# Merging the two 64-key tails of a neighbourhood-attention value product into one block-diagonal matmul

## The reference

```
q, k, v = split(h @ w_qkv)                      # 16 heads of 64 features
# a query in grid column c sees all 8 rows and a clamped window of 16 columns
scores = q . k + bias[head, row offset, column offset]
p = softmax(scores)                             # over 8 x 16 keys
out = (p @ v) @ w_o
```

## Time and profile before

| | |
|---|---|
| three runs, us | 1041.26, 1042.48, 1043.23 (median 1042.48) |
| span of the profiled execution, us | 1041.8 |
| busy: PE, PE weight loads, DVE, ACT, POOL | 99%, 87%, 81%, 57%, 10% |
| attention loop on PE | about 553 to 690 us from the span's start |
| transposes (line 953) | 128 records |
| values (line 975) | 256 records |

### The profile page before, as it was taken

One profiled execution on the slowest core, in us unless ns is written; L12 is line 12 of the kernel. 1 busy time (PEld: TensorE's weight loads), 2 busy tenths in 40 slices (PEclk: granted clock), 3 DMA queues, 4 the chain that ended last, 5 costly groups with the idle time before them and its releaser, 6 DMA issues.

```text
span 1041.8 us, 15414 instructions
## 1 busy us (share of the span) xinstructions
PE 1032.3 (99%) x6104; PEld 905.4 (87%) x6104; DVE 846.8 (81%) x1185; ACT 598.4 (57%) x836; POOL 103.6 (10%) x158
## 2 busy tenths in 40 slices
PE   9999999999999999999999999999999999999997
PEld 8888888988998998998878888889888988988985
DVE  5876688699899689688987767797799798698697
ACT  6222347665584574575765655547664674674675
POOL 3453001000000000000113000000000000000003
PEclk9999999999999999999999999999999999999999
DMA  7998568326745645633998733157056547447423
GB/s 247 375 375 300 141 165 254 108 42 207 204 132 176 177 128 177 181 97 102 372 249 249 215 90 114 55 191 274 1 122 205 163 133 202 150 134 202 147 51 111
DMA packets 36998, 182.71 MB, mean 175 GB/s; under 512 B 5760, under 2 KB 5888, under 8 KB 22848
## 3 DMA queue, kind: packets, MB, share of 16 engines
q1 hardware_dynamic: 23184, 108.57, 28.8%
q0 software_dynamic: 13456, 72.64, 28.3%
q10 hardware_dynamic: 288, 0.52, 0.2%
HBM read 136.93 MB, written 27.32 MB: 158 GB/s over the span
## 4 chain that ended last, share of the span: by engine, by line
PE 93%; DVE 4%; DMA 1%; ACT 1%; issue 1%; POOL 0%; DVEq 0%; POOLq 0%; ACTq 0%
PE bank L770 29%; PE bank L771 29%; PE bank L772 29%; DMA raw<-sevens 1%; PE bank L975 1%; PE bank L953 1%; DVE w_l L1514 1%; PE bank L938 1%; PE bank L793 1%; DVE xs L1661 1%; PE bank L997 0%; DVE big L1970 0%; ACT big L1156 0%; DVE a_l L1727 0%; ACT w_h L1128 0%
## 5 line engine op out<-in xcount | busy, mean ns | idle before, releaser
L1128 ACT ACTIVATE w_h<-big 128x1024 fp32r<-128x1024 f32 x210 | 221.7, 1058 | 216.0 <-PE bank L772 215.0
L770 PE MATMUL bank<-a_h,w_h 128*128 128x256 f32 (+1 forms) x892 | 295.0, 331 | 0.0
L772 PE MATMUL bank<-a_h,w_l 128*128 128x256 f32 (+1 forms) x892 | 292.9, 328 | 0.0
L771 PE MATMUL bank<-a_l,w_h 128*128 128x256 f32 (+1 forms) x892 | 292.8, 328 | 0.0
L1514 DVE TENSOR_TENSOR w_l<-big,w_h 128x1024 fp32r<-128x1024 f32 x210 | 252.0, 1225 | 21.8 <-ACT w_h L1128 21.8
L770 PE MATMUL bank<-w_h,hx 128*128 128x512 f32 x568 | 222.1, 391 | 0.8 <-ACT big L1376 0.4
L771 PE MATMUL bank<-w_l,hx 128*128 128x512 f32 x568 | 221.2, 389 | 0.0
L772 PE MATMUL bank<-w_h,hx 128*128 128x512 f32 x568 | 221.0, 389 | 0.0
L770 PEld LDWEIGHTS bank<-a_h,w_h 128*128 128x128 f32 x892 | 169.6, 190 | 15.8 <-issue 0.2
L772 PEld LDWEIGHTS bank<-a_h,w_l 128*128 128x128 f32 x892 | 169.6, 190 | 15.0
L771 PEld LDWEIGHTS bank<-a_l,w_h 128*128 128x128 f32 x892 | 169.6, 190 | 14.7 <-issue 0.2
(11 more groups left out here) (193 smaller groups left out, 1253.6 us busy)
## 6 DMA issues: line engine op xcount, KB each, us to landing
big<-blocks SPq DMA_DIRECT2D x56, 1024.0 KB, 5.0
big<-big POOLq DMA_DIRECT2D x30, 1024.0 KB, 7.0
raw<-weights SPq DMA_DIRECT2D x52, 512.0 KB, 6.6
raw<-t_sums SPq DMA_DIRECT2D x16, 512.0 KB, 3.7
t_sums<-sevens POOLq DMA_DIRECT2D x6, 1024.0 KB, 12.6
t_sums<-t_sums POOLq DMA_DIRECT2D x6, 1024.0 KB, 12.2
raw<-sevens SPq DMA_DIRECT2D x12, 512.0 KB, 7.8
bias_tiles<-big POOLq DMA_DIRECT2D x8, 632.0 KB, 9.3
```

The costliest lines, as they stand in the source:

```text
L770: nc.tensor.matmul(dst, sh, mh, start=start, stop=False, skip_group_check=again)
L771: nc.tensor.matmul(dst, sh, ml, start=False, stop=False, skip_group_check=again)
L772: return nc.tensor.matmul(dst, sl, mh, start=False, stop=stop, skip_group_check=again)
L1128: nc.scalar.activation(wh_all[:, w % SLOTS, :], src, ACT.Copy).then_inc(w_hi, 1)
```

## The change

The 192-key block of each half is split differently for the two heads. The even head's main chunk is its first 128 keys and its tail the last 64; the odd head's main chunk is its last 128 keys and its tail the first 64. `prob` is laid out so that the even head's tail and the odd head's tail are neighbours in the middle, 128 columns. They are transposed together in one transpose (columns 384 to 511 of the first bank) and multiplied by one 128 x 128 tile `v_pair_tail`, block diagonal: the even head's features of its 64 tail tokens in rows 0 to 63, the odd head's in rows 64 to 127, zero elsewhere. A round then has seven transposes and seven matmuls; the merged one writes all 128 partitions and comes first in `values`. DVE copies 384 columns in place of 512; ACT still 512.

On POOL, the memset of the last shifted copy covers 128 partitions, a second memset of 128 x 1024 is added behind the wait for V, the DMA that filled the last shifted copy is gone, and four DMAs per feature half fill the tail tiles with every second head's 64 features (256 bytes each, 64 KB a DMA). `v_in` counts ten DMAs in place of seven, and `h_raw` moves by 1024 columns, since other V tiles stay in use.

```diff
+TPOSED = ((0, 0), (1, 0), (1, 1))
-        V_AT = [(v_tile[0], v_tile[1]), (v_shift[0], v_shift[1]), (v_shift[1], v_shift[2]),
-                (v_shift[2], v_shift[3])]
+        V_MAIN = {0: (v_tile[0], v_shift[0]), 3: (v_shift[2], v_tile[3])}
+        V_AT = {1: (v_shift[0], v_shift[1]), 2: (v_shift[1], v_shift[2])}
+        v_pair_tail = {0: big[:, 17 * D:18 * D], 3: v_shift[3]}
+        TAIL_OF = {0: (v_tile[1][0:HD, :], v_tile[0][0:HD, :]), 3: (v_tile[3][HD:P, :], v_tile[2][HD:P, :])}
+        def heads(t, par_):
+            return t.rearrange("p (j h f) -> p j h f", h=2, f=HD)[:, :, par_, :]
-        h_raw = big[:, 8192:10240].rearrange("p (k t) -> p k t", k=4)
+        h_raw = big[:, 7168:9216].rearrange("p (k t) -> p k t", k=4)
...
-            at = score_at(half, n)
-            offset = par_ * PROB_W // 2
-            return slice(offset + at.start, offset + at.stop)
+            width = ROWS * KEYS[HALVES[half][n]][1]
+            first = (PROB_W // 2 - width, 0)[n] if par_ == 0 else (PROB_W // 2, PROB_W - width)[n]
+            return slice(first, first + width)
...
-            pool.memset(v_shift[3][HD:P, :], 0.0).then_inc(shift_zero, 1)
+            pool.memset(v_pair_tail[3], 0.0).then_inc(shift_zero, 1)
             pool.wait_ge(v_add, 4)
+            pool.memset(v_pair_tail[0], 0.0).then_inc(shift_zero, 1)
             for half in range(2):
                 f = slice(512 * half, 512 * half + 512)
                 for s in range(4):
                     if s:
                         pool.dma_start(v_shift[s - 1][HD:P, f], v_tile[s][0:HD, f]).then_inc(v_in[half], 16)
-                    pool.dma_start(v_shift[s][0:HD, f], v_tile[s][HD:P, f]).then_inc(v_in[half], 16)
+                    if s < 3:
+                        pool.dma_start(v_shift[s][0:HD, f], v_tile[s][HD:P, f]).then_inc(v_in[half], 16)
+                pool.wait_ge(shift_zero, 2)
+                for par_ in range(2):
+                    rows = slice(HD * par_, HD * par_ + HD)
+                    for b, tail in v_pair_tail.items():
+                        pool.dma_start(heads(tail[rows, f], par_), heads(TAIL_OF[b][par_][:, f], par_)).then_inc(v_in[half], 16)
...
+                tails = slice(PROB_W // 2 - HD, PROB_W // 2 + HD)
+                nc.tensor.transpose(tposed[0][:, 3 * P:4 * P], prob[half][:, tails], ident[:])
                 for par_ in range(2):
-                    for n, b in enumerate(HALVES[half]):
-                        at = prob_at(half, par_, n).start
-                        for c, (_, width) in enumerate(CHUNKS_OF[b]):
-                            t = 2 * n + c
-                            last = nc.tensor.transpose(tposed[par_][0:width, P * t:P * t + P],
-                                                       prob[half][:, at + P * c:at + P * c + width], ident[:])
+                    for t, (n, c) in enumerate(TPOSED):
+                        at = prob_at(half, par_, n).start + (P * c if n else HD * par_)
+                        width = CHUNKS_OF[HALVES[half][n]][c][1] if n else P
+                        last = nc.tensor.transpose(tposed[par_][0:width, P * t:P * t + P], prob[half][:, at:at + width], ident[:])
...
-                    pe.wait_ge(shift_zero, 1)
-                    pe.wait_ge(v_in[j // 4], 16 * 7)
-                for n, b in enumerate(HALVES[half]):
-                    for c in range(2):
-                        for par_ in range(2):
+                    pe.wait_ge(v_in[j // 4], 16 * 10)
+                dst = attn_last if j == KT - 1 and half else attn_out
+                first = HALVES[half][0]
+                nc.tensor.matmul(dst[:, P * first:P * first + P], v_pair_tail[first][:, P * j:P * j + P],
+                                 probT[half][:, 3 * P:4 * P], start=True, stop=False, skip_group_check=True)
+                for t, (n, c) in enumerate(TPOSED):
+                    b = HALVES[half][n]
+                    for par_ in range(2):
...
-                    act.wait_ge(v_in[0], 16 * 7)
-                    act.wait_ge(v_in[1], 16 * 7)
+                    act.wait_ge(v_in[0], 16 * 10)
+                    act.wait_ge(v_in[1], 16 * 10)
...
-                nc.vector.tensor_copy(probT[half][:, 512:1024], tposed[1][:]).then_inc(pt_ready_o, 1)
+                nc.vector.tensor_copy(probT[half][:, 512:896], tposed[1][:, 0:3 * P]).then_inc(pt_ready_o, 1)
```

More of the change, by code:

```diff
@@ L965, in values @@
                         pe.wait_ge(attn_free, j - 4)
-                    pe.wait_ge(shift_zero, 1)
-                    pe.wait_ge(v_in[j // 4], 16 * 7)
-                for n, b in enumerate(HALVES[half]):
-                    for c in range(2):
-                        for par_ in range(2):
[L971 to L976, removed]
+                    pe.wait_ge(v_in[j // 4], 16 * 10)
[6 more added lines that the diff above has]
+                    for par_ in range(2):
+                        rows = slice(HD * par_, HD * par_ + HD)
+                        feats = slice(P * j + HD * par_, P * j + HD * par_ + HD)
+                        at = 512 * par_ + P * t
+                        keys = V_AT[b][c] if n else V_MAIN[b][par_]
+                        last = nc.tensor.matmul(dst[rows, P * b:P * b + P], keys[:, feats], probT[half][:, at:at + P],
+                                                start=(n, c) == (1, 0), stop=(n, c) != (1, 0), skip_group_check=True)
                 last.then_inc(pv_done, 1)
```

## The result

The changed kernel takes 1047.57 us (median of 5 runs, 1045.91 to 1050.21) against 1043.23 us for the kernel before (5 runs). The medians lie 4.3 us apart; the ratio over the runs is 1.0050 (5.2 us), 95% interval 1.0038 to 1.0061: slower, by 4 to 6 us. The profiled execution spans 1045.8 us.

The account below looks back on a forecast made before the run. PE, busy 99% of the span, was taken as the bound. Transposes -1.53, switches +1.8, DVE's end -0.2 and stall +1.5 gave +1.6 us on the median of 1042.48: 1044.1, range 1040.5 to 1047.4.

Parts of the forecast that it names:

- Transposes: PE, attention rounds: one of eight transposes fewer, 0.109 us each, 1.74 us in all, 1.53 of it counted behind the stall.
- Values, gain 0: PE's values: the merged matmul takes 0.22 us, as did the even and odd pair it replaces, so no gain.
- Switches of the array's form, 0.30: PE's values: half 1's merged matmul adds one exit and entry of the 64-column form, seven at 0.30 us, 2.1 us.
- V's tiles, stall +1.5: POOL's V DMAs: the last lands near 574.4 instead of 572.9, stalling PE 1.5 us, the tenth DMA's delay included.
- Rival 1: Last V DMA lands at 578.0, PE stands 5 us before pair 1: +5.2 us, 1047.6; chance 0.37, shared with stalls over 2.
- Copies out of PSUM: DVE copies 384 columns for 512: worth nothing in the loop, 0.2 us less behind the last pair.
- The bias tile, no term: POOL's bias tile of pair 2: lands 1 to 2 us later, but its use is 1.5 later too, so nothing added.

Follow-up runs that it names:

- e11: Changed kernel with second memset earlier, ACT copying four tails, half 1's merged matmul (pairs 0 to 6) behind the next pair's scores; output wrong: 1042.52 us, ratio 0.9991.
- e12: Changed kernel with second memset earlier, ACT copying four tails, both halves' merged matmul behind the first 64-column pair: 1046.56 us, ratio 1.0035 to the kernel before.
- e9: Changed kernel with twelve unused full-width matmuls put in PE's wait before the values of pair 0: 1046.00 us, ratio 1.0034 to the kernel before.
- e4: Kernel before, PE untouched, with the added memset, six tail DMAs into a spare region and waits raised to ten DMAs: 1048.16 us, ratio 1.0051.
- e14: e11 with half 1's bank opened once and ACT's V wait and pair 0 copy behind pair 1's exponentials: 1040.49 us, ratio 0.9976 to the kernel before.
- e1: Changed kernel with the second memset moved ahead of POOL's wait for V: 1046.84 us, ratio 1.0044 to the kernel before.

## Why the prediction was wrong

The forecast was 1044.1 us, inside what a measurement tells from no change, with a range up to 1047.4. It measured 1047.57, and slower beyond the noise. Step by step:

- **Transposes**: right. Seven in 0.76 us (587.33 to 588.09), 0.109 each; with the changes of form taken away, the period falls by 0.25 us for the 0.22 forecast.
- **Values, gain 0**: right. In e11, where the merged matmuls cost no extra change of form, the period differs from the old one by the transposes and 0.03 us.
- **Switches of the array's form, 0.30**: right in mechanism, mis-sized by a little: 0.35 and 0.33 by e11 and e12. The loop's balance is +0.1 us a pair. The rule of the Trainium skill (TensorEngine Tiling (Array Packing), Key Properties), that a change of tiling mode drains the engine, agrees with these prices, though no row shows the draining itself; the price is larger than what the merging saves (0.25 a pair).
- **V's tiles, stall +1.5**: this is the step that failed, in two ways. First, I let the landing of the last DMA set the sum and took the tenth as part of it, at "the median landing of 4.7". It was issued at 563.2, which is the forecast 564.1 less the shift of the whole stretch, and took 6.7 us. The median mixes copies issued into an empty queue (2.2 us at 558.1) with those issued into a full one, and the trace before had 7.0 us for the two issued at 563.28 and 563.79: with that row the forecast would have been 564.1 + 7.0 = 571.1, 3.2 us behind the start of values, against the 2.8 that came. The second wait (ACT's, to 576.0, where 574.4 was forecast) was later than forecast too and hid behind the first. Second, a stall was priced at its own length. The clock was not in the sum at all: it cost 1.6 us more, by the profile after and by e9, and e4 shows both costs with the old PE work.
- **Rival 1** gave 1047.6, which is the measured time by luck, for it rests on the wrong wait: it priced the last landing 5.1 us late. That landing came 3.7 us later in the attention than before (23.6 us behind the first scores for 19.9), and PE did not stand between the q projection and line 953's counterpart.
- **Copies out of PSUM**: nothing in the loop, as forecast. The 0.2 us put for the end are not seen: from the last scores to the projection behind the last values it is 20.59 us for 20.83, and the 0.24 less are all but filled by PE's own two transposes (0.22).
- **The bias tile, no term**: right for the changed kernel, where PE is late itself. Once the stalls are gone (e14), it can be the next wait.

With the terms as measured (stall 2.8, clock 1.6, seven changes of form at 0.34, since pair 0's lies behind the stall that came, and nothing for DVE) the sum is -1.53 + 2.4 + 4.4 = +5.3 us, against 5.2 by the ratio and by the stretch in the profiles, and 4.3 between the medians.

## What to carry to other kernels

When a change adds transfers ahead of a first use, list every count that some engine waits for, and land each by the rows of the queue as full as it will then be; a median over a queue that was empty at first is too kind, and the landing of the copy issued at the same moment stood in the trace. Price a stall of PE with what the clock does behind it, and put a full-width matmul among narrow column tiles only where full-width work already stands: the same merged matmul cost 0.35 us a pair or nothing, by its place.

## What the runs showed of the hardware that was not expected

- After PE had been idle for 2.8 us, the granted clock fell to 0.50 (1.2 GHz) just as work began again, and stayed there for some 3 us; in e4 this came behind a wait of 2.0 us (0.87 and 0.70 in the two windows), and in e1, behind 2.3 us, it lasted nearly 7 us. Behind the waits of 1.7 us in e11 and e14 the granted clock stayed at 1.00. So the changed kernel's stall cost over one and a half times its length, and those of 1.7 us cost 1.9.
- Two matmuls of 64 stationary columns on different halves of the array's columns take the time of one: 16 pairs of records in 1.96 us, where 32 in a row at 0.109 would need 3.5. Merging such a pair into one full-width matmul gains nothing on PE.
- 256-byte pieces within SBUF are joined into larger packets when POOL issues the DMA (no small packet more for the pieces of eight such DMAs; 16 for every DMA more, of 64 or 128 KB alike) and are single packets when SP does (2048 more, and 161 GB/s from engines 94% busy, where the changed kernel's moved about 260).
